# One decoder layer step: where the prompt attention issues the second half of the scores of the unit two ahead, before or behind the value products

## The reference

```python
logits = jnp.einsum('bqhd,bqkhd->bqhk', q, kg) * (HEAD_DIM ** -0.5)
logits = jnp.where(valid[:, :, None, :], logits, NEG_INF)
p = jax.nn.softmax(logits, axis=-1)
out = jnp.einsum('bqhk,bqkhd->bqhd', p, vg)
```

## Time and profile before

| | |
|---|---|
| median of 3 runs | 1414.7 us (1411.8 to 1416.4) |
| the profiled execution | 1413.2 us, its span 1411.3 us |
| TensorE busy | 1355.4 us (96%), weight loads 1256.1 us (89%) |
| VectorE, ScalarE, GpSimd busy | 638.0, 461.9, 524.6 us (45%, 33%, 37%) |
| share of TensorE in the chain that ended last | 79% |
| mean granted TensorE clock | 0.991 of full |

### The profile page before, as it was taken

One profiled execution on the slowest core, in us unless ns is written; L12 is line 12 of the kernel. 1 busy time (PEld: TensorE's weight loads), 2 busy tenths in 40 slices (PEclk: granted clock), 3 DMA queues, 4 the chain that ended last, 5 costly groups with the idle time before them and its releaser, 6 DMA issues.

```text
span 1411.3 us, 24909 instructions
## 1 busy us (share of the span) xinstructions
PE 1355.4 (96%) x9384; PEld 1256.1 (89%) x9384; DVE 638.0 (45%) x1419; ACT 461.9 (33%) x1017; POOL 524.6 (37%) x512
## 2 busy tenths in 40 slices
PE   5989999999998999989999999999999999999998
PEld 4849999985667898768999999999999999999997
DVE  6278997668874222135433232232332322323345
ACT  6345887637765222232320110110201102002034
POOL 5325973434422112312433333333333333333510
PEclk9999999998999999999999999999999999999999
DMA  6421113300012976870211111111111111111203
GB/s 181 89 63 41 47 53 122 92 16 1 2 31 67 289 228 182 245 236 16 60 46 46 46 45 46 46 46 46 46 46 46 46 45 46 46 46 45 73 3 123
DMA packets 129401, 107.05 MB, mean 76 GB/s; under 512 B 19736, under 2 KB 108440, under 8 KB 129279
## 3 DMA queue, kind: packets, MB, share of 16 engines
q1 hardware_dynamic: 120581, 99.00, 23.5%
q10 hardware_dynamic: 8050, 4.63, 1.1%
q0 software_dynamic: 656, 1.84, 0.6%
HBM read 94.57 MB, written 9.20 MB: 74 GB/s over the span
## 4 chain that ended last, share of the span: by engine, by line
PE 79%; DVE 4%; SPq 3%; issue 2%; ACT 2%; POOL 1%; DMA 0%; DVEq 0%; ACTq 0%; POOLq 0%
PE bank L1842 72%; PE bank L2018 2%; PE bank L2080 2%; SPq L527 2%; SPq L528 1%; DVE junk L1502 1%; ACT sjunk L1032 1%; PE bank L1888 1%; DVE prob L1593 1%; DVE hn_lo L1726 1%; DVE lack L1506 1%; POOL rdenb L788 0%; PE bank L2159 0%; PE bank L2322 0%; PE bank L2044 0%
## 5 line engine op out<-in xcount | busy, mean ns | idle before, releaser
L837 POOL TENSOR_TENSOR w_hi<-w_raw,zero 128x1024 fp32r<-128x1024 f32 x60 | 114.3, 1905 | 463.6 <-PE bank L1842 428.0
L1842 PE MATMUL bank<-hn_hi,w_hi 128*128 128x384 f32 (+1 forms) x768 | 250.7, 326 | 3.1 <-issue 2.3
L1842 PE MATMUL bank<-hn_lo,w_hi 128*128 128x384 f32 (+1 forms) x768 | 248.9, 324 | 0.0
L1842 PE MATMUL bank<-hn_hi,w_lo 128*128 128x384 f32 (+1 forms) x768 | 247.9, 323 | 0.0
L1269 ACT ACTIVATE relu<-relu 128x384 f32<-128x384 f32 (+1 forms) x96 | 47.9, 499 | 550.9 <-DVE relu L1776 550.9
L1842 PE MATMUL bank<-hid_hi,w_hi 128*128 128x384 f32 (+1 forms) x672 | 217.8, 324 | 0.0
L1842 PE MATMUL bank<-hid_lo,w_hi 128*128 128x384 f32 (+1 forms) x672 | 217.2, 323 | 0.0
L1842 PE MATMUL bank<-hid_hi,w_lo 128*128 128x384 f32 (+1 forms) x672 | 216.3, 322 | 0.0
L1791 DVE TENSOR_TENSOR acc<-bank,acc 128x384 f32<-128x384 f32 x168 | 86.9, 523 | 207.5 <-PE bank L1842 207.5
L1842 PE MATMUL bank<-xn_hi,w_hi 128*128 128x384 f32 (+1 forms) x456 | 150.9, 331 | 1.6 <-POOL w_lo L628 0.9
L626 POOL TENSOR_TENSOR w_hi<-w_raw,zero 128x256 fp32r<-128x256 f32 x108 | 68.7, 636 | 224.9 <-PE bank L1842 190.2
(11 more groups left out here) (261 smaller groups left out, 2349.3 us busy)
## 6 DMA issues: line engine op xcount, KB each, us to landing
w_raw<-in_w_ff_dram SPq DMA_DIRECT2D x64, 512.0 KB, 3.8
page<-in_cache_k_dram SPq DMA_DIRECT2D x64, 256.0 KB, 3.4
page<-in_cache_v_dram SPq DMA_DIRECT2D x64, 256.0 KB, 3.1
w_raw<-in_w_in_dram SPq DMA_DIRECT2D x18, 512.0 KB, 3.7
xrow<-in_x_prompt_dram SPq DMA_DIRECT2D x8, 512.0 KB, 8.1
w_raw<-in_w_out_dram SPq DMA_DIRECT2D x8, 512.0 KB, 4.4
xblk<-in_x_prompt_dram SPq DMA_DIRECT2D x8, 512.0 KB, 4.9
out_dram<-yrow SPq DMA_DIRECT2D x8, 512.0 KB, 2.7
```

The source lines that it names most:

```text
L837: nc.gpsimd.tensor_tensor(w_hi[n[0] % 2][:, :], w_raw[n[0] % 2][:, :], zero_w, ALU.add).then_inc(s_whi, 1)
L1842: return nc.tensor.matmul(out, lhsT, rhs, start=start, stop=stop)
```

## The change

In the rounds called `early` (units with two halves that have a unit two ahead: u = 16 to 29, 14 rounds) half 1 of the scores of unit u+2 is issued last, behind `pv(u)`, instead of between `p_T(2u+1)` and `pv(u)` (or `spread_T`, in even rounds). Half 0 stays between the two `p_T`. No instruction is added or removed, no wait is added, and the lists of the other engines are the same.

```diff
@@ -2058,13 +2058,13 @@
                 if early:
                     qk(u + 2, (0,))
                 p_T(2 * u + 1)
-                if early:
-                    qk(u + 2, (1,))
-                elif u + 2 < NU:
+                if u + 2 < NU and not early:
                     qk(u + 2)
                 if u % 2 == 0 and u >= 2:
                     spread_T(u // 2 - 1)
                 pv(u)
+                if early:
+                    qk(u + 2, (1,))
             spread_T(NU // 2 - 1)
```

## The result

The changed kernel takes 1426.9 us (median of 4 runs, 1425.3 to 1427.9) against 1414.9 us before; the ratio is 1.0086 with a 95% interval of 1.0067 to 1.0106. The change makes the kernel 12 us slower; 1425.6 was forecast, in a range of 1420 to 1432. A later comparison of the same two kernels gave 1.0096 (1.0076 to 1.0115).

The account below looks back on a forecast made before the run. TensorE's own list was taken to bound rounds 16 to 29; 8.5 us of uncovered waits plus 2.4 us of late VectorE and GpSimd work made 1413.2 + 10.9 = 1424.1, with 1.5 for the median 1425.6 us, range 1420 to 1432.

Parts of the forecast that it names:

- Rounds 16 to 29 are bound by TensorE's list, and the scores cover the wait for the last copy: TensorE idles 0.9 of 74.40 us there; moving half 1 uncovers its wait before the value products, 8.5 us in sum.
- bare term: Each round's growth from the uncovered wait for the last copy alone, 0.42 to 0.95 us, 8.5 us over rounds 16 to 29.
- What is late next: Half 1 reaches VectorE late, delaying copies or spreads in rounds 17, 18, 21, 22, 23; about 2.4 us, from 0 to 4.8.
- half of 0.63, and the 0.11: Round 20 into 21: half 1's first product reaches VectorE some 0.45 us after the value products end, an estimate.
- q: Length of half 1's two products on TensorE: 0.42, 0.63, 0.84, 1.06 us for 128, 256, 384, 512 columns.
- X: The moment the value products end, from which half 1's arrival at VectorE was timed in rounds 20 to 22.
- The end of block 5 in round 22 hangs on GpSimd: Round 22's spread waits over 1.2 us for GpSimd's copy of the denominators; value products 0.8 us later.
- Exponentials, banks and SyncE cost nothing; all later work moves by the full loss: No added wait from these three; SyncE's transfer some 3 us nearer the attention's end; later stages keep their length.
- The bare wait alone: Rival for rounds 16 to 29: VectorE and GpSimd follow in time, +8.5 us, 1423; inside the main case, no separate chance.
- a gain: Rival: moved products fill other TensorE gaps in the 14 rounds, at most 0.9 us, 1414; real gain 1%.
- A fall of the clock: Rival: new TensorE gaps bring one to three half-clock stretches, +16 to +26 us, 1431 to 1441; chance 6%.
- q in every round, 11.0 us: Ceiling for the uncovered wait in the 14 rounds, as if the scores had covered nothing else and hidden wholly there.

Follow-up runs that it names:

- the split pair: Changed kernel, but the first head's half-1 product stays in front of the value products and only the second head's goes behind; ratio 1.0083 to the kernel before.

## Why the prediction was right, and where it was off

- *Rounds 16 to 29 are bound by TensorE's list, and the scores cover the wait for the last copy.* Right. The nine rounds for which nothing more was forecast (16, 19, 20 and 24 to 29) grew by 5.53 us in sum, where the terms gave 5.58. The moves of the last six rounds alone gave 4.09 for 4.07. Round 19 stands behind a selection and still cost no more than its bare term: VectorE's copy was late there, but it let the value products go 0.94 us after the transposes ended, as ScalarE's copy would have (0.93).
- *What is late next, 2.4 us.* Right in mechanism and in its places (rounds 17, 18, 21, 22, 23), too small: it measured 3.5 us (6.42 in these five rounds, less 2.90 bare). The mis-sized step is "half of 0.63, and 0.11": the first product of half 1 is not there at half the pair's time. It is there q + 0.11 after X, when the pair has ended, which is 0.74 us and not 0.45 for 256 columns (393.66 to 394.40), and by the same sum 0.95 for 384 columns. The rows of the kernel before couldn't show it, because VectorE never waited there for a half 1. By this step alone (half of each pair's time, an estimate) the five rounds would be short by 0.2, 0.2, 0.3, 0.3 and 0.4 us; they were short by 0.11, 0.20, 0.28, 0.22 and 0.36, 1.2 us in sum, so the step is large enough for all of it. The same step shows in round 29: VectorE's idle time ahead of its copy fell from 2.33 us to 0.83, by 1.5 us and not the 1.1 of the prediction, which still left enough. The Trainium skill ("TensorE: Matmul & The Clock Gate", section "Part 3: Packing small matmuls — row/col tiling") says that matmuls placed in different row groups of the array run at the same time. The two heads lie in partitions 0 to 63 and 64 to 127, and the split pair agrees with it: 1.05 us for one, 1.06 for both.
- *The end of block 5 in round 22 hangs on GpSimd.* Right: the spread waited 1.41 us for a copy of 2.37.
- *Exponentials, banks and SyncE cost nothing; all later work moves by the full loss.* Right: the last two rounds and the rest have their old lengths. SyncE's transfer of prompt rows now goes out 10.6 us ahead of the attention's end (453.38 to 464.0) in place of 12.5, 1.9 us nearer and not 3.
- *The rivals.* The bare wait alone is refuted by the five rounds, a gain by the table. A fall of the clock didn't come: it was 1.00 in the window in both profiles of the changed kernel, with idle gaps of up to 1.5 us. That this rival was worth a chance is shown outside the window. In round 6 TensorE waits 1.49 us for GpSimd in five of the profiles; in three of them round 7 then ran at 1.00, and in two at 0.57 and 0.58.
- The ceiling "q in every round, 11.0 us" for the bare part was not reached, but it is what the split pair costs.

That the median came out 1.3 us from the forecast says little by itself: the medians give a loss of 12.0 and 11.6 us in two comparisons, with an interval of 9.5 to 15 us in the first. The rounds are what shows that the sum was 1.1 us short (10.8 for 11.95), and where.

## What to carry to other kernels

Work that stands between a producer and an in-order engine's wait for its result is worth the smaller of its own length and that wait; moving it behind the wait costs this sum, which can be read off the places where nothing stands in between. Then follow what was moved: its consumer is late too, and whatever stands behind the consumer in its list (here mask pieces and the next copy) may reach the same engine one round on. And a queue's slack has to be judged as a whole: taking one collision away, or moving a long piece elsewhere in the list, only gave the wait to another round.

## What the runs showed of the hardware

- Two float32 products with 64 rows each, in the two halves of the array, cost what one costs: 1.05 us alone and 1.06 for the pair at 512 columns. The first reduction of a pair starts 0.11 us after the end of the pair (0.74 us behind its start at 256 columns).
- A group of such products has a fixed part of 0.21 us beside 0.21 us for each 128 columns; two groups put next to each other pay it once (1.91 against 2.12 us).
- GpSimd's copy of 128x256 takes 0.40 us alone, and 2.37 beside VectorE's running sum of 2.33; beside a selection with two SBUF inputs of 0.85 it takes 0.96. In each case it ends 0.20 to 0.26 us behind VectorE's operation.
- Idle gaps of 0.5 to 1.5 us, one in each round of 5 to 7 us, left TensorE's granted clock at 1.00 through all 86 us, in two profiles. It is no rule that such gaps are safe: behind a wait of 1.49 us in round 6 the clock stayed at 1.00 in three profiles and fell to 0.57 and 0.58 for round 7 in two.
